# Routed experts: all eight ranked before the first, four of 128 slots and four of 64, six small groups at the end

## What is computed

```python
logits = (xt @ w_router + b_router).astype(jnp.float32)      # 256 tokens, 8 experts
top_val, top_idx = lax.top_k(logits, TOP_K)                  # TOP_K = 2
gates = jax.nn.softmax(top_val, axis=-1)
...
hb = jax.nn.silu(xb @ w1[e]) * (xb @ w3[e])                  # w1, w3: 1024 x 3584 for each expert
return hb @ w2[e]                                            # w2: 3584 x 1024
```

## Time and profile before

| | |
|---|---|
| median of 3 runs | 1446.25 us (1446.16 to 1446.78) |
| the profiled execution's own time | 1446.92 us |
| its span in the profile | 1445.2 us |
| PE busy / weight loads | 1422.1 / 1206.0 us |
| DVE busy | 1282.8 us |
| ACT busy | 1016.5 us |
| moved by DMA | 506.27 MB, mean 350 GB/s |

### The profile page before, as it was taken

One profiled execution on the slowest core, in us unless ns is written; L12 is line 12 of the kernel. 1 busy time (PEld: TensorE's weight loads), 2 busy tenths in 40 slices (PEclk: granted clock), 3 DMA queues, 4 the chain that ended last, 5 costly groups with the idle time before them and its releaser, 6 DMA issues.

```text
span 1445.2 us, 19311 instructions
## 1 busy us (share of the span) xinstructions
PE 1422.1 (98%) x7352; PEld 1206.0 (83%) x7352; DVE 1282.8 (89%) x1277; ACT 1016.5 (70%) x992; POOL 71.5 (5%) x112
## 2 busy tenths in 40 slices
PE   9999999999999999999999999999999999999996
PEld 5799889878889988888888888888888788888884
DVE  6899889977777768999999999999999999999996
ACT  2774454443667358778888788888888888888874
POOL 5000000000000000010000000000000010000010
PEclk9999999999999999999999999999999999999998
DMA  9849849987453857999999999999999999999993
GB/s 372 322 178 352 322 179 379 390 345 291 172 211 119 304 209 269 378 410 356 415 421 421 419 382 422 415 422 420 421 417 420 421 416 419 419 422 421 418 372 153
DMA packets 74645, 506.27 MB, mean 350 GB/s; under 512 B 8908, under 2 KB 9036, under 8 KB 17074
## 3 DMA queue, kind: packets, MB, share of 16 engines
q1 hardware_dynamic: 69986, 490.91, 84.9%
q0 software_dynamic: 4560, 14.07, 2.8%
HBM read 499.00 MB, written 7.88 MB: 351 GB/s over the span
## 4 chain that ended last, share of the span: by engine, by line
PE 88%; DVE 5%; ACT 3%; issue 3%; DMA 1%; SPq 0%; DVEq 0%; ACTq 0%
PE ps L2005 22%; PE ps L2007 21%; PE ps L2006 21%; PE ps L2493 6%; PE ps L2494 6%; PE ps L2530 2%; PE ps L2066 2%; DVE lo L1300 2%; ACT hi L755 2%; PE ps L2533 1%; PE ps L2230 1%; PE ps L2213 1%; DVE lo L1272 1%; ACT hi L739 1%; DMA raw<-in_w_first_dram 1%
## 5 line engine op out<-in xcount | busy, mean ns | idle before, releaser
L1300 DVE TENSOR_TENSOR lo<-raw,hi 128x2048 fp32r<-128x2048 f32 x245 | 552.5, 2286 | 22.3 <-ACT hi L755 22.1
L755 ACT ACTIVATE hi<-raw 128x2048 fp32r<-128x2048 f32 x245 | 461.1, 1919 | 29.2 <-DMA raw<-in_moe_w_dram 21.4
L2005 PE MATMUL ps<-hi,hT_hi 128*128 128x512 f32 (+3 forms) x896 | 348.3, 389 | 4.2 <-DVE hT_lo L1326 2.0
L2007 PE MATMUL ps<-hi,hT_lo 128*128 128x512 f32 (+3 forms) x896 | 342.5, 382 | 0.0
L2006 PE MATMUL ps<-lo,hT_hi 128*128 128x512 f32 (+3 forms) x896 | 342.1, 382 | 0.0
L1300 DVE TENSOR_TENSOR lo<-r,hi 128x2048 fp32r<-128x2048 f32 x91 | 206.6, 2286 | 8.1 <-ACT hi L755 7.9
L1272 DVE TENSOR_TENSOR lo<-raw,hi 128x2048 fp32r<-128x2048 f32 (+3 forms) x83 | 177.0, 2146 | 37.8 <-ACT hi L739 29.7
L2005 PEld LDWEIGHTS ps<-hi,hT_hi 128*128 128x128 f32 x896 | 168.3, 188 | 39.1 <-issue 4.3
L2007 PEld LDWEIGHTS ps<-hi,hT_lo 128*128 128x128 f32 x896 | 168.2, 188 | 32.0
L2006 PEld LDWEIGHTS ps<-lo,hT_hi 128*128 128x128 f32 x896 | 168.4, 188 | 30.0 <-issue 0.2
L755 ACT ACTIVATE hi<-r 128x2048 fp32r<-128x2048 f32 x91 | 173.0, 1920 | 12.5 <-DMA r<-in_moe_w_dram 6.3
(11 more groups left out here) (361 smaller groups left out, 1779.5 us busy)
## 6 DMA issues: line engine op xcount, KB each, us to landing
raw<-in_moe_w_dram SPq DMA_DIRECT2D x245, 1024.0 KB, 10.0
r<-in_moe_w_dram SPq DMA_DIRECT2D x91, 1024.0 KB, 9.8
raw<-in_w_ada_dram SPq DMA_DIRECT2D x40, 1024.0 KB, 6.5
raw<-in_w_fd_dram SPq DMA_DIRECT2D x11, 1024.0 KB, 6.7
raw<-in_w_ga_dram SPq DMA_DIRECT2D x8, 1024.0 KB, 5.6
raw<-in_w_gb_dram SPq DMA_DIRECT2D x8, 1024.0 KB, 5.2
raw<-in_w_ab_dram SPq DMA_DIRECT2D x8, 1024.0 KB, 4.8
raw<-in_w_o_dram SPq DMA_DIRECT2D x8, 1024.0 KB, 6.5
```

Of the source, the lines that this page charges most:

```text
L755: act.activation(high_of(s), raw_of(r), ACT.Copy).then_inc(hi_done, 1)
L1300: dve.tensor_tensor(low_of(s), raw_of(r), high_of(s).bitcast(f32), ALU.subtract).then_inc(raw_done, 1)
L2005: pe.matmul(o, wh, mh, start=first, stop=False)
L2007: return pe.matmul(o, wl, mh, start=False, stop=last)
```

## The change

All eight experts are ranked before any of their weights is loaded. `expert_order` now runs on DVE between the second `top_two` and `first_slots(1)`, on the counts that PE makes right after the second selection; ties are broken in one operation (8 x count - number). Item 0 is the expert with most rows. `item_slots` makes the slot tables there too, and `item_gates` the gate tables in `first_x`, after `moe_lo(2)`. SP waits for `experts_ready` ahead of item 0 as well. ACT and DVE convert chunks 0 to 2 among and behind the steps of item 0's rows (`first_x` on DVE), where before chunks 0 and 1 were converted at the end of the mixer. `LARGE` goes from 5 to 4: four large items, four small ones (28 and 28 units, before 35 and 21). Units 0 to 4 are large, then small and large alternate up to unit 48, and units 50 to 55 are small. The last item is a small one of 16 rows, so the last unit's steps are those of `small_silu`, `small_hidden`, `small_hi`, `small_lo`.

```diff
+END_DRAIN = (4, 0, 1, 2)
-LARGE = 5
+LARGE = 4
-SMALL_AT = [7 + 9 * k // 4 for k in range((EXPERTS - LARGE) * NG)]
+SMALL_AT = [5 + 2 * k if k < 22 else 28 + k for k in range((EXPERTS - LARGE) * NG)]
-END = LARGE - 1
+END = EXPERTS - 1
-PREPS = (0, 5, 1, 2, 6, 3, 7, 4)
+PREPS = (0, 4, 1, 5, 2, 6, 3, 7)
...
@@ SP
-                if g == 0 and i:
+                if g == 0:
                     sp.wait_ge(experts_ready, 1)
                     expert[i] = sp.value_load(info[0:1, i:i + 1], min_val=0, max_val=EXPERTS - 1)
...
@@ ACT
             upto("m1.wo3")
-            moe_hi(0, 1)
...
             m.then_inc(xn_ready, 1)
-            moe_hi(2)
...
-                moe_hi(after)
+                if n < UNITS_ALL - 1:
+                    moe_hi(after)
...
                 if n == UNITS_ALL - 1:
-                    hidden_hi(n)
+                    moe_hi(after)
+                    small_silu(n)
+                    act.wait_ge(used, NW + unit_chunk(n - 1, "w2", 1) + 1)
+                    small_hi(n)
                 moe_hi(after + 1)
...
                 for b in (2 * h, 2 * h + 1):
                     first_high(b)
+                moe_hi(h)
+            moe_hi(2)
...
@@ DVE
-            moe_lo(0, 1)
...
+            def expert_order():
+
+                dve.wait_ge(count_full, 2)
+                link(dve.scalar_tensor_tensor(orank, ps[:, R_BANK[1], 32:32 + E], float(E), eidx[:, :], ALU.mult, ALU.subtract))
+                link(dve.tensor_tensor(cmp[:, 0], orank.unsqueeze(1).to_broadcast([P, E, E]), orank.unsqueeze(2).to_broadcast([P, E, E]),
+                                       ALU.is_gt))
+                link(dve.reduce_sum(order, cmp[:, 0], AX))
+                link(dve.tensor_tensor(perm, order.unsqueeze(1).to_broadcast([P, E, E]),
+                                       eidx[:, :].unsqueeze(2).to_broadcast([P, E, E]), ALU.is_equal))
+                link(dve.tensor_tensor(ee, perm, eidx[:, :].unsqueeze(1).to_broadcast([P, E, E]), ALU.mult))
+                link(dve.reduce_sum(info_f[:, 0:E], ee, AX))
+                dve.tensor_copy(info[:, 0:E], info_f[:, 0:E]).then_inc(experts_ready, 1)
...
             top_two(1)
+            expert_order()
             first_slots(1)
+            item_slots()
...
-                    first_low(h)
-                first_low(2)
-                first_low(3)
+                    first_low(2 * h)
+                    first_low(2 * h + 1)
+                    moe_lo(h)
                 moe_lo(2)
-                counted()
-                link(dve.tensor_copy(pg[:, :], slot_x[:, :, 0]))
+                gates()
+                item_gates()
+                picked(0, 0)
                 for t in range(T):
                     m = one_hot(t, 1.0)
                 m.then_inc(first_hot, 1)
-                gates()
...
@@ PE
+            pe.wait_ge(sel_ready, 2)
+            count(R_BANK[1], 32, [(ones, 0), (ones, 1)])
+            count(0, 40, [(ones, 0), (before, 1)])
+            keep_busy(10, X_BANK[1])
             pe.wait_ge(hot0_ready, 1)
             gather_first(0, 0)
...
+            keep_busy(9, X_BANK[1])
...
                 unit_up(n, "w1")
...
-                if n == 1:
+                if n == 0:
                     slot_rows(0)
```

More of the change, by code:

```diff
@@ L695, in gather_rows @@
                     pool.wait_ge(m_gath, 2 * PREP_OF[before_] + 2)
-                if i >= LARGE and PREP_OF[i] > 4:
+                if i >= LARGE and i > LARGE + 1:
                     pool.wait_ge(rows_out, ROWS_OUT[before_ - 1])
@@ L1629, in first_slots @@
             def first_slots(t):
-                dve.wait_ge(count_full, t + 1)
-                slot = slot_x[:, t, :]
-                link(dve.scalar_tensor_tensor(slot, ps[:, 0, 32 + t * E:32 + (t + 1) * E], 1.0, sel[:, t, :], ALU.add, ALU.mult))
-                dve.tensor_scalar(r4[:, t * P:(t + 1) * P], slots1[:, :], slot_x[:, t, 0:1], rstd[:, T + t:T + t + 1],
-                                  ALU.is_equal, ALU.mult).then_inc(m_pos if t else hot0_ready, 1)
+                dve.wait_ge(count_full, 2 * t + 1)
@@ new lines, in first_slots @@
+                link(dve.scalar_tensor_tensor(slot_x[:, t, :], ps[:, 0, 32 + t * E:32 + (t + 1) * E], 1.0, sel[:, t, :], ALU.add, ALU.mult))
+            def expert_order():
[9 more added lines that the diff above has]
+                dve.tensor_copy(info[:, 0:E], info_f[:, 0:E]).then_inc(experts_ready, 1)
+                dve.wait_ge(experts_ready, 1)
+                dve.tensor_copy(cnt, ps[:, R_BANK[1], 32:32 + E]).then_inc(ov_ready, 1)
+                dve.wait_ge(ov_ready, 1)
@@ new lines, in item_slots @@
+            def item_slots():
+                for t in range(T):
+                    m = dve.tensor_tensor(cmp[:, t], perm, slot_x[:, t, :].unsqueeze(1).to_broadcast([P, E, E]), ALU.mult)
+                link(m)
+                for t in range(T):
+                    m = dve.reduce_sum(pos_tab[:, t, 0:E], cmp[:, t], AX)
+                link(m)
+                for t in range(T):
+                    dve.tensor_scalar(r4[:, t * P:(t + 1) * P], slots1[:, :], pos_tab[:, t, 0:1], rstd[:, T + t:T + t + 1],
+                                      ALU.is_equal, ALU.mult).then_inc(m_pos if t else hot0_ready, 1)
+                dve.wait_ge(m_pos, 1)
+                dve.tensor_scalar(pos_tab[:, :, 0:E], pos_tab[:, :, 0:E], -1.0, None, ALU.add)
+                link(dve.tensor_scalar(slot_x, slot_x, -1.0, None, ALU.add))
@@ L1663, in _ @@
             m.then_inc(ex_in, 1)
-            dve.wait_ge(m_pos, 1)
-            link(dve.tensor_scalar(slot_x, slot_x, -1.0, None, ALU.add))
             def gates():
@@ L1755, in one_hot, with gate_hot @@
                                          ALU.is_equal, ALU.mult)
-            def gate_hot(t):
-                return dve.tensor_scalar(r4[:, 256 + t * P:256 + (t + 1) * P], slots[:, :], pg[:, t:t + 1], vals[:, t, 2:3],
+            def gate_hot(t, small=False):
+                return dve.tensor_scalar(r4[:, 256 + t * P:256 + (t + 1) * P], (slots_s if small else slots)[:, :], pg[:, t:t + 1], vals[:, t, 2:3],
                                          ALU.is_equal, ALU.mult)
@@ L1902, in unit @@
                     rows(ROWS_AT[n])
-                if n == UNITS_ALL - 1:
-                    hidden(n)
                 moe_lo(after)
                 if n == UNITS_ALL - 1:
-                    hidden_lo(n)
+                    small_hidden(n)
+                    small_lo(n)
                 elif not SMALL[n]:
@@ L2437, in _ @@
             route(1, 1)
+            pe.wait_ge(sel_ready, 2)
+            count(R_BANK[1], 32, [(ones, 0), (ones, 1)])
+            count(0, 40, [(ones, 0), (before, 1)])
+            keep_busy(10, X_BANK[1])
             pe.wait_ge(hot0_ready, 1)
             gather_first(0, 0)
-            keep_busy(1, X_BANK[1])
-            pe.wait_ge(sel_ready, 2)
-            count(0, 40, [(ones, 0), (before, 1)])
-            gather_first(0, 1)
             pe.wait_ge(m_pos, 1)
             gather_first(1, 0)
+            gather_first(0, 1)
             gather_first(1, 1)
-            count(R_BANK[1], 32, [(ones, 0), (ones, 1)])
-            keep_busy(2, X_BANK[1])
+            keep_busy(9, X_BANK[1])
             def gather(i, part, bank=7):
@@ L2465, in slot_rows @@
                     pe.wait_ge(idx_ready, p)
-                if p >= 3:
+                if p >= 2:
                     pe.wait_ge(m_xf, 2 * p - 2)
                 for t in range(T):
-                    m = pe.matmul(ps[:, 7 if p < 3 else 3, 0:4], r4[:, t * P:(t + 1) * P], vals[:, t, :], start=(t == 0), stop=(t == T - 1))
+                    m = pe.matmul(ps[:, 7 if p < 2 else 3, 0:4], r4[:, t * P:(t + 1) * P], vals[:, t, :], start=(t == 0), stop=(t == T - 1))
                 m.then_inc(idx_full, 1)
@@ L2661, in drain @@
                         pe.wait_ge(m_yc, i * 2 - (EXPERTS - 1) + q + 1)
-                    scatter(i, q, DRAIN[q])
+                    scatter(i, q, (END_DRAIN if i < EXPERTS else DRAIN)[q])
             for n in range(UNITS_ALL):
```

59 lines of the change are left out of this document (18 added, 41 removed).

## The result

| | before | after |
|---|---|---|
| median | 1447.29 us (6 runs, 1446.16 to 1449.60) | 1459.99 us (6 runs, 1459.40 to 1464.09) |
| ratio | | 1.0090, 95% interval 1.0074 to 1.0106 |
| profiled execution | 1446.92, span 1445.2 | 1462.21, span 1460.5, mean clock 0.991 |

The changed kernel is slower by 12.7 us in the medians, where I had forecast 3. In the profiled executions it is 15.3, because the one of after lies 2.2 above its median. In the last series (e8_fill, b2_hold, e9_best, e10_pre) 13 of the 35 runs of the kernel before and 5 of the 12 of b2_hold took some 10 us longer than the others, so beside each ratio of that series I give the distance of the other runs' medians, 1447.1 us for the kernel before and 1455.2 for b2_hold.

What follows compares the result with a forecast made beforehand. The weight stream was taken as the bound: last landing 1414.4 + 4.1 + 1.5 = 1420.0 us, plus 28.15, gives a 1448.2 us span, 3.0 above before. On the median that made 1449.2, rounded up to 1449.5; range 1441 to 1456.

Steps and rivals of the forecast that it cites:

- DVE's steps: Behind the third `moe_lo`, in unit 0: 18 small steps in place of eleven, taking 3.6 us.
- the two waits: PE in unit 0: 2.8 us for chunk 1's conversion, 3.5 us for item 0's indices.
- the rest: From the start of PE's last group of scatters to the end of the span: 15.75 us, unchanged from before.
- PE's cheaper units are not on the path: Seven units go from 17.1 to 12.4 us, 33 us less PE work, but the stream is 27 us longer.
- up to there the 11 chunks hide that a large unit is 2.2 us longer than its transfers: Up to chunk 38, slots and `lo` buffers cover the large units' lag; only 2.3 us are lost there.
- start loss of 4.1 us: Stream starved in the first units: 2.3 us at chunk 38 and 1.8 us from DVE in units 5 and 6.
- a floor of 653.2 under the issue of chunk 38: Chunk 38 can't be issued before unit 4's end at 651 us plus a `lo` of 2.2.
- Rival 3: Router's hand-over to unit 0: half clock slows 24 to 36 matmuls, costing 5.4 to 8 us; 1455 to 1458; 11%.
- The second step: The end: last landing at 1420.0 us, then 28.15 us to the end of the span, no shorter with a small item.
- Last landing: 1414.4 + 4.1 + 1.5: Last chunk: 1414.4 us if perfectly fed, plus 4.1 start loss and 1.5 middle loss, 1420.0 us.
- The ceiling of 435 GB/s: Fabric limit from the skill page; at it 336 chunks would take 810 us in place of 837.
- The rival that hung on it: Rival 2: PE is the bound if the stream can exceed 421 GB/s, so cheaper units count; 1427.5 us; 9%.

Runs made afterwards that it cites:

- e8_fill: Changed kernel with PE's three holes at the hand-over filled by keep-busy matmuls (eight, ten, eight): 1459.72 us, ratio 1.0067 to the kernel before.
- b2_hold: Kernel before with item 0's first load waiting for the first one-hot rows and chunks 0 to 2 converted as in the changed kernel: 1455.55 us, ratio 1.0062.
- e9_best: Changed kernel with ten fewer keep-busy matmuls before the gather, new unit order, earlier small steps, filled holes, extra slots kept until chunk 326: 1455.28 us, ratio 1.0028.
- e10_pre: Changed kernel with item 0's weights loaded ahead and ten fewer keep-busy matmuls before the first gather: 1453.17 us, ratio 1.0014 to the kernel before.
- e4: Changed kernel with item 0's gates to one-hot rows moved behind chunk 4 and its index matmuls from unit 0 to unit 1: 1463.79 us, ratio 1.0109.
- e1: Changed kernel with the hidden rows' small steps one chunk earlier where a small unit follows a small one: 1459.28 us, ratio 1.0086 to the kernel before.
- e5: Changed kernel with the two extra raw slots leaving the ring at chunk 331 in place of 320: 1466.48 us, ratio 1.0117 to the kernel before.
- e6: Changed kernel with earlier small steps and a new order: four large units first, small ones sooner, four small at the end: 1459.04 us, ratio 1.0075.
- e7: Changed kernel with ten fewer keep-busy matmuls before the gather, extra slots until chunk 331, new unit order and earlier small steps: 1457.23 us, ratio 1.0074.
- e3: Changed kernel with item 0's expert number fixed in the program, its weights loaded and first chunks converted ahead: 1455.34 us, ratio 1.0059 to the kernel before.
- e2: Changed kernel with 10 instead of 20 keep-busy matmuls between the counts and the first gather: 1459.13 us, ratio 1.0085 to the kernel before.

## Why the prediction was wrong

**What held.** First issue 555.25 (555.6), first landing 559.7 (560.4), the full stretch at 418 to 419 GB/s, the row traffic 7.2 MB or 17.2 us (16). DVE's steps took 3.1 us (3.6), the two waits 2.5 and 2.2 (2.8 and 3.5). PE's last scatter starts at 1444.74, 13.3 us behind the last landing (12.4), and the rest is 15.76 (15.75). The last chunk's `hi` starts 7 us after its landing:

```profile
1438.35 1.91 ACT hi L756
1440.28 2.30 DVE lo L1307
...
1444.74 2.75 PE ps L2651 x6
```

And the premise: PE's cheaper units are not on the path. From landing 72 to the end before takes 705.5 us, after 705.7.

**The step that failed** is "up to there the 11 chunks hide that a large unit is 2.2 us longer than its transfers", with its start loss of 4.1 us. By my sum landing 72 is at 560.4 + 179.3 + 3.1 (rows) + 0.9 + 4.1 = 747.8; it was at 754.8. Up to chunk 11 the stream ran as the sum has it (landing 588.0; 560.4 + 11 x 2.49 = 587.8). Chunks 12 to 38 then took 76.5 us in place of 67.2, where the sum lets the stream run full and puts a floor of 653.2 under the issue of chunk 38. That chunk was issued at 659.6, when `lo` of chunk 31 ended: PE had left unit 4 at 654.1, 3.1 us later than in the sum, and DVE's order added 3.3, since a table's small steps and two other conversions stood ahead of that `lo`.

The 11 buffers would hide a lag if they were filled ahead, and they are not. SP issues each chunk at the instant at which `moe_lo` frees a raw slot, and the chunk lands soon after. `moe_lo` in turn follows PE, directly or behind ACT: from 585 to 755 us ACT's copy of the turned rows (L1052) waits 22.8 us for PE, DVE's `lo` 6.2 for ACT's `hi`, and PE itself stands 2.1 us in all, none of it for a landing. From issue to landing in the changed kernel, 585 to 690 us, and then in the full stretch, 870 to 1350:

```profile
DMA to landing us min/median/max: 4.7/7.2/9.3
...
DMA to landing us min/median/max: 9.3/12.5/14.3
```

7.2 us at 2.49 a chunk is three chunks in flight, 12.5 is five. (SP's wait for `lo` doesn't tell the two apart: it is 88.8 us of the first 105 and 392.7 of the other 480.) So PE is the bound from its first expert matmul until small units have let it catch up (save where DVE holds it, as in unit 0 and in e4's unit 1), and whatever delays PE there is handed on to the end. The table shows it: the distance from the 264th matmul to landing 72 is 117.9 to 118.2 us in the eight kernels of the changed order while the 264th itself moves by 11.8; 119.7 to 120.0 in the three of the old order while it moves by 8.1; 114.4 to 114.7 in the three of the new one. The term should have read: landing 72 is late by what the 264th matmul is late, 16.8 us, less 1.7, which I put down to the first small unit coming two units sooner. The earlier trace rows had a sign of the loss in the kernel before: the prediction reads 415 to 422 GB/s "from slice 18 on", but that begins with slice 20, and slices 18 and 19 have 410 and 356.

My own numbers for PE, 581.8 for the end of unit 0 and 634 for that of unit 3, were some 3 us short of what came (584.9, 636.9). With the rule of the table they give landing 72 at 634 + 118 = 752. Of the 7.0 us missed there, 4 are the rule and 3 PE: the gather behind the keep-busy matmuls (2.0) and the half clock (1.5) less what my waits had too much. Rival 3 named the right place and the right direction and sized it by the half clock alone, 24 to 36 matmuls; it was eight.

**The second step** is the end. The sum lets the last chunks run at full speed ("Last landing: 1414.4 + 4.1 + 1.5"). They lose 4.5 us beside their bytes (23 chunks and 2.2 MB of row traffic, 62.6 us), as they had lost 4.1 before, which stood as 391 GB/s in the earlier trace rows. From landing 72 to the last the sum has 672.2 us, the trace 676.6; behind it 28.15 and 29.1. Together 5.3 us. The sum thus gave the smaller groups a gain of 5 us over the kernel before behind landing 72, and there was 0.2 of loss. 7.0 + 4.4 + 0.9 is the whole miss, 1448.2 to 1460.5.

In the kernel before this holds to the end. PE's waits from 585 to 1430 us in before, all of them:

```profile
PE ps L2005 <- DVE bT_lo L1833: 2.5, 5, 0.7
PE ps L2479 <- DMA c_rows<-rows_x,token_row: 0.8, 1, 0.8
```

and the first two in after:

```profile
PE ps L2496 <- DVE bT_hi L1849: 9.6, 4, 4.9
PE ps L2008 <- DVE bT_lo L1840: 7.5, 12, 0.9
```

PE had 3.3 us to spare in 845, beside a stream that was full as well. The smaller groups turn PE's work into waits, and the stream's length stays.

**What stays open** is who owns the last 23 chunks. The small steps (e1), the ring (e5), the read-back's time (e9) and fewer small units at the end (e6, e7, e9) were each taken away or moved, and they still take 66.6 to 67.6 us against 62.5 to 63.1 for their bytes. Half clock isn't it either: e6 has no slow matmul between landings 312 and 335, and 66.6 us. That each stands ready behind the other is a guess; it is 1.6 us of the difference. Open is as well what the 18 keep-busy matmuls behind the gather cost once the weights are at hand (e3, e10), since no run has fewer.

**The ceiling of 435 GB/s**, which the prediction took from the Trainium skill: nothing ran at it. From 550 us on the highest window of 10 us was 426 in after and 428 in before, and the full stretch stayed at 419. The rival that hung on it, PE as the bound in the middle, did not come.

## What to carry to other kernels

A buffer hides a delay only if it is full when the delay comes: read the time from issue to landing, not the number of slots. If each issue stands right behind the release of a slot and the landing comes soon after, the consumer is the bound, even beside a stream at 90% of its rate, and each us that it starts late is a us of the end. When a change touches both a start and a steady stretch, forecast by differences from marks of the kernel before (first matmul, a landing in the full stretch, last landing, end), not by a new sum from zero: a sum leaves out the losses that the old kernel already had, and books them as a gain.

## What the runs showed of the hardware

A hole of 1.9 us in PE's work (549.97 to 551.90) was followed by a granted clock of 0.74 to 0.87 from 555 to 560 us in six executions (after, e2, e5, e6, e7, e10) and by 1.00 in three (e1, e3, e4) in which PE has the same hole ahead of the same work. 20 keep-busy matmuls took 6.25 us in the one case and 4.56 in the other. With the hole filled (e8, e9) it stayed at 1.00. In unit 0 holes of 2.5 and 2.2 us were followed by matmuls 0.43 us apart in place of 0.23. The Trainium skill, "TensorE: Matmul & The Clock Gate", section "What's actually happening", says that the number of slow matmuls differs from run to run of the same kernel; the trace agrees, with 8 to 14 of them (0.54 us and longer, where full clock shows 0.39) among the first 48 in executions whose unit 0 is the same (e1, after, e5, e6).

At the end, where PE waits in each small unit, the same happens (clock 0.66 from 1400 to 1410 in after). From the last landing to the end it takes 29.0 to 32.1 us in seven kernels that do the same work there, and the clock goes with it: the three of 29.0 and 29.1 (after, e3, e8) have 8 matmuls of 512 columns over 0.55 us in it, the four of 30.6 to 32.1 (e2, e4, e5, e10) have 13 to 16.
